# Splitting fp32 weights by whole units: 1024 columns per instruction instead of 512, with the last round and the first stage reordered

## The reference

```python
h = rms_norm(x, norm_w[l])
proj = h @ w_in[l]                                   # 512x2048 @ 2048x6144
q, k, v, g_a, u_p, g_p = jnp.split(proj, [A, 2 * A, 3 * A, 4 * A, 4 * A + P], axis=-1)
attn = diff_attention(q, k, v, ...)                  # two softmaxes per head, p0 - lam * p1
pool = multiscale_pool(u_p, w_pool[l], pool_scale[l])
mixed = jnp.concatenate([attn * jax.nn.silu(g_a), pool * jax.nn.silu(g_p)], axis=-1)
x = x + mixed @ w_out[l]                             # 512x2048 @ 2048x2048
```

## Time and profile before

| what | value |
|---|---|
| median of 3 runs | 789.1 us (788.91 to 791.22) |
| the profiled execution | 789.31 us, span 787.5 us |
| TensorE busy | 775.0 us (98%) |
| VectorE busy | 551.9 us (70%) |
| ScalarE busy | 381.7 us (48%) |
| GpSimd busy | 31.6 us (4%) |
| DMA | 106.22 MB, mean 135 GB/s |

### The profile page before, as it was taken

How to read it: one execution, slowest core, us unless ns; L and a number is a source line. 1 busy time by engine, 2 the same in 40 slices (tenths; PEclk the granted TensorE clock), 3 DMA queues, 4 the chain that set the end, 5 groups by cost and what they waited for, 6 DMA issues and landing times.

```text
span 787.5 us, 9660 instructions
## 1 busy us (share of the span) xinstructions
PE 775.0 (98%) x3470; PEld 638.1 (81%) x3470; DVE 551.9 (70%) x861; ACT 381.7 (48%) x649; POOL 31.6 (4%) x42
## 2 busy tenths in 40 slices
PE   9999999999999999999999999999999889999997
PEld 8878888888888888888888888888788678888886
DVE  5443235887874787785488789458877869887796
ACT  5373234444373444445444437444444756655552
POOL 0010000000000000000000000000000003222200
PEclk9999999999999999999999999999999999999999
DMA  9844323282121336212146322222722169999972
GB/s 333 331 129 132 104 88 101 80 215 77 58 80 54 120 108 173 81 53 81 54 134 154 113 63 71 71 91 80 214 69 66 54 196 266 275 277 264 210 169 107
DMA packets 67079, 106.22 MB, mean 135 GB/s; under 512 B 5344, under 2 KB 46560, under 8 KB 66528
## 3 DMA queue, kind: packets, MB, share of 16 engines
q1 hardware_dynamic: 60288, 86.72, 34.6%
q0 software_dynamic: 4736, 16.78, 10.9%
q10 hardware_dynamic: 2016, 2.18, 0.9%
HBM read 95.17 MB, written 4.19 MB: 126 GB/s over the span
## 4 chain that ended last, share of the span: by engine, by line
PE 85%; DVE 5%; ACT 4%; DMA 3%; SPq 2%; issue 1%; POOL 0%; DVEq 0%; ACTq 0%; POOLq 0%
PE ps L460 83%; DMA raw<-in_w_in 2%; PE ps L587 2%; PE ps L455 1%; ACT probs L807 1%; DMA q_stack<-q_low 1%; SPq L291 1%; DVE probs L1049 1%; ACT at_hi L662 1%; DVE w_lo L907 1%; ACT diff L815 0%; DVE diff L1097 0%; DVE probs L1047 0%; DVE wp_lo L1100 0%; DVE h_lo L934 0%
## 5 line engine op out<-in xcount | busy, mean ns | idle before, releaser
L907 DVE TENSOR_TENSOR w_lo<-raw,w_hi 128x512 fp32r<-128x512 f32 x240 | 163.1, 688 | 167.0 <-ACT w_hi L688 91.3
L460 PE MATMUL ps<-h_hi,w_hi 128*128 128x512 f32 x640 | 251.0, 392 | 0.0
L460 PE MATMUL ps<-h_lo,w_hi 128*128 128x512 f32 x640 | 249.4, 390 | 0.0
L460 PE MATMUL ps<-h_hi,w_lo 128*128 128x512 f32 x640 | 171.2, 389 | 0.0
L688 ACT CAST w_hi<-raw 128x512 fp32r<-128x512 f32 x149 | 90.4, 620 | 161.5 <-PE ps L460 160.7
L460 PEld LDWEIGHTS ps<-h_hi,w_lo 128*128 128x128 f32 x640 | 120.1, 188 | 25.1
L460 PEld LDWEIGHTS ps<-h_hi,w_hi 128*128 128x128 f32 x640 | 120.1, 188 | 24.7
L460 PEld LDWEIGHTS ps<-h_lo,w_hi 128*128 128x128 f32 x640 | 120.2, 188 | 24.6
L460 PE MATMUL ps<-w_hi,h_hi 128*128 128x512 f32 x352 | 122.4, 392 | 2.4 <-DVE h_lo L934 1.3
L460 PE MATMUL ps<-w_hi,h_lo 128*128 128x512 f32 x352 | 121.4, 389 | 0.0
L460 PE MATMUL ps<-w_lo,h_hi 128*128 128x512 f32 x352 | 121.4, 389 | 0.0
(11 more groups left out here) (143 smaller groups left out, 790.0 us busy)
## 6 DMA issues: line engine op xcount, KB each, us to landing
raw<-in_w_in SPq DMA_DIRECT2D x96, 512.0 KB, 3.6
raw<-in_w_out SPq DMA_DIRECT2D x12, 512.0 KB, 3.7
raw<-in_w_out POOLq DMA_DIRECT2D x12, 512.0 KB, 17.2
wide_b<-in_w_out POOLq DMA_DIRECT2D x12, 512.0 KB, 19.1
x_rows<-in_x SPq DMA_DIRECT2D x4, 1024.0 KB, 13.8
tall<-in_w_out SPq DMA_DIRECT2D x8, 512.0 KB, 13.0
tall<-in_w_out POOLq DMA_DIRECT2D x8, 512.0 KB, 23.1
mixed<-in_x_cols SPq DMA_DIRECT2D x3, 1024.0 KB, 13.3
```

What stands on the lines that cost most here:

```text
L460: last = nc.tensor.matmul(dst, lhs, rhs, start=first and i == 0, stop=final and i == len(pairs) - 1, skip_group_check=True)
L907: nc.vector.tensor_tensor(w_lo[:, slot, :], src, w_hi[:, slot, :].bitcast(F32), ALU.subtract).then_inc(w_lo_ready, 1)
```

## The change

ACT and DVE split a whole unit in one instruction each, 1024 columns wide, into two adjacent slots. In the first stage and the rounds this is done at even steps, for halves m+2 and m+3 (before: at each step for half m+3); ACT waits until all halves before m are used. Both semaphores rise by 2 at once. In the projection it is done at even halves.

Other edits: `WARM` from 22 to 16. SP loads one tile of x rows after each of the units 1 to 4, instead of two after each of the units 0 and 1; `x_stats` in steps 11 to 14 instead of 9 to 12, and DVE's factors at step 15 instead of 14. SP moves k before its wait for unit 6 instead of after it. In the last round the forms of pass 0 come a step earlier on ACT (34 to 36), those of pass 1 at 43 to 45 on ACT and 44 to 46 on DVE (before: 38 to 40 on both), the pool is mixed and its form made in step 41 before the weights' split (before: step 42); the two Silus swap places.

```diff
         def form_count(p, pair):
-            if p < 2:
-                return (7 + p) if pair == KP // 2 - 1 else 3 * p + pair + 1
             return (KP // 2) * p + pair + 1
...
                     load_in(Q, nxt - UNITS, 0)
-                if u < 2:
-                    load_x_row(2 * u)
-                    load_x_row(2 * u + 1)
+                if 1 <= u <= ST:
+                    load_x_row(u - 1)
...
                 for unit in range(UNITS - G_UNITS if last_round else UNITS):
+                    if unit == 6:
+                        move_k(r)
                     if unit in (7, 8):
...
                         load_in(Q, j, r + 1)
-                    if unit == 6:
-                        move_k(r)
...
-            def split_first(n):
-                unit, part = divmod(n, 2)
-                if part == 0:
-                    act.wait_ge(raw_in[unit % RAW_SLOTS], (unit // RAW_SLOTS + 1) * 16)
-                if n >= W_SLOTS:
-                    act.wait_ge(w_used, n - W_SLOTS + 1)
-                nc.scalar.copy(w_hi[:, n % W_SLOTS, :], raw[:, unit % RAW_SLOTS, part * 512:part * 512 + 512]
-                               ).then_inc(w_hi_ready, 1)
+            def split_pair(slot, src):
+                nc.scalar.copy(w_hi[:, slot:slot + 2, :].rearrange("p s n -> p (s n)"), src).then_inc(w_hi_ready, 2)
+            def split_first(unit):
+                act.wait_ge(raw_in[unit % RAW_SLOTS], (unit // RAW_SLOTS + 1) * 16)
+                if unit >= 2:
+                    act.wait_ge(w_used, 2 * unit - 2)
+                split_pair(2 * unit % W_SLOTS, raw[:, unit % RAW_SLOTS, :])
...
-                unit, part = divmod(m, 2)
-                if part == 0:
-                    act.wait_ge(raw_in[unit % RAW_SLOTS],
-                                r * (UNITS // RAW_SLOTS * 16) + (V_UNITS + unit) // RAW_SLOTS * 16 + 16)
-                act.wait_ge(w_used, r * HALVES + before(m) - W_SLOTS + 1)
-                nc.scalar.copy(w_hi[:, m % W_SLOTS, :], raw[:, unit % RAW_SLOTS, part * 512:part * 512 + 512]
-                               ).then_inc(w_hi_ready, 1)
+                unit = m // 2
+                act.wait_ge(raw_in[unit % RAW_SLOTS],
+                            r * (UNITS // RAW_SLOTS * 16) + (V_UNITS + unit) // RAW_SLOTS * 16 + 16)
+                act.wait_ge(w_used, r * HALVES + before(m) - 2)
+                split_pair(m % W_SLOTS, raw[:, unit % RAW_SLOTS, :])
...
                 if p == 0:
-                    u, part = divmod(h, 2)
-                    if part == 0:
-                        act.wait_ge(raw_in[u % RAW_SLOTS], ((IN_HALVES // 2 + u) // RAW_SLOTS + 1) * 16)
-                    src = raw[:, u % RAW_SLOTS, part * 512:part * 512 + 512]
+                    u = h // 2
+                    act.wait_ge(raw_in[u % RAW_SLOTS], ((IN_HALVES // 2 + u) // RAW_SLOTS + 1) * 16)
+                    src = raw[:, u % RAW_SLOTS, :]
                 else:
-                    j, part = divmod(hj, 2)
-                    if part == 0:
-                        act.wait_ge((None, wide_in, wide_added, tall_in, wide_added, tall_added, wide_added)[p][j],
-                                    PASS_LANDED[p])
-                    src = w_tile(p, j)[:, part * 512:part * 512 + 512]
-                act.wait_ge(w_used, IN_HALVES + h - W_SLOTS + 1)
-                nc.scalar.copy(w_hi[:, h % W_SLOTS, :], src).then_inc(w_hi_ready, 1)
+                    j = hj // 2
+                    act.wait_ge((None, wide_in, wide_added, tall_in, wide_added, tall_added, wide_added)[p][j],
+                                PASS_LANDED[p])
+                    src = w_tile(p, j)
+                act.wait_ge(w_used, IN_HALVES + h - 2)
+                split_pair(h % W_SLOTS, src)
...
                             nc.scalar.copy(q_stack[rows, c, h], wk(0)[rows, h]).then_inc(qk_hi_ready, 1)
-                    if not last_round or m + 3 < 8 + HALVES - G_HALVES:
-                        split_high(m + 3, r)
-                    else:
-                        split_form_w(m - 37 if m < 41 else 2 * m - 78)
+                    if last_round and m == 41:
+                        form_high(0, KP // 2 - 1)
+                    if m % 2 == 0 and (not last_round or m < 38):
+                        split_high(m + 2, r)
+                    elif last_round and m in (38, 40):
+                        split_form_w(m - 38)
+                    elif last_round and m >= 41:
+                        split_form_w(2 * m - 78)
                     if m == 10:
...
                         nc.scalar.copy(wp_hi, wp_raw[:, :]).then_inc(wp_hi_ready, 1)
-                    if last_round and 35 <= m < 38:
-                        form_high(0, m - 35)
+                    if last_round and 34 <= m < 37:
+                        form_high(0, m - 34)
                     if m == 40:
...
                         nc.scalar.preload_act_table(ACT.Silu)
-                        act.wait_ge(evacuated, r * 3 + 1 + START)
-                        nc.scalar.activation(gate[:, :, :], gate[:, :, :], ACT.Silu).then_inc(gate_ready, 1)
                         act.wait_ge(evacuated, r * 3 + 3 + START)
                         nc.scalar.activation(wk(0), wk(0), ACT.Silu).then_inc(pool_gate_ready, 1)
+                        nc.scalar.activation(gate[:, :, :], gate[:, :, :], ACT.Silu).then_inc(gate_ready, 1)
                         nc.scalar.preload_act_table_set(LN_EXP)
...
                         squares(head_out[:, :], hsq_hi, ps[:, OB, :])
-                    if last_round and 38 <= m < 41:
-                        form_high(1, m - 38)
+                    if last_round and 43 <= m < 46:
+                        form_high(1, m - 43)
                     if m == 42:
                         rstd(head_out[:, :], ps[:, S0, :], 2 * HEAD_DIM, r * 4 + 3)
-                    if last_round and m == 42:
-                        form_high(0, KP // 2 - 1)
                     if m == 46:
...
                                        ).then_inc(pool_placed, 1)
-                    if last_round and m >= 41:
-                        split_form_w(2 * m - 77)
...
                 x_high(q)
-                split_first(2 * q)
-                split_first(2 * q + 1)
+                split_first(q)
             for n in range(1, HALVES):
...
                     nc.scalar.activation(lam_exp[:, :], lam_sum[:, :], ACT.Exp).then_inc(lam_exped, 1)
-                split_first(n + 3)
-                if 9 <= n <= 12:
-                    x_stats(n - 9)
+                if n % 2 == 0:
+                    split_first(n // 2 + 1)
+                if 11 <= n <= 14:
+                    x_stats(n - 11)
                 if KT < n <= KT + ST:
...
                         nc.scalar.copy(corner_part(b), ps[:, OUT_BANKS[1][b], :]).then_inc(first_copied, 1)
-                split_form_w(h)
+                if h % 2 == 0:
+                    split_form_w(h)
                 if hj in (4, 7, 10, 13) and p + 1 < PASSES:
...
                 dve.wait_ge(w_hi_ready, count)
-                nc.vector.tensor_tensor(w_lo[:, slot, :], src, w_hi[:, slot, :].bitcast(F32), ALU.subtract
-                                        ).then_inc(w_lo_ready, 1)
-            def raw_half(n):
-                return raw[:, (n // 2) % RAW_SLOTS, (n % 2) * 512:(n % 2) * 512 + 512]
+                nc.vector.tensor_tensor(w_lo[:, slot:slot + 2, :].rearrange("p s n -> p (s n)"), src,
+                                        w_hi[:, slot:slot + 2, :].rearrange("p s n -> p (s n)").bitcast(F32),
+                                        ALU.subtract).then_inc(w_lo_ready, 2)
+            def raw_pair(n):
+                return raw[:, (n // 2) % RAW_SLOTS, :]
             def split_low(m, r):
-                split_rest(m % W_SLOTS, raw_half(m), r * HALVES + before(m) + 1)
+                split_rest(m % W_SLOTS, raw_pair(m), r * HALVES + before(m) + 2)
...
                 p, hj = divmod(h, P_HALVES)
-                src = raw_half(h) if p == 0 else w_tile(p, hj // 2)[:, (hj % 2) * 512:(hj % 2) * 512 + 512]
-                split_rest(h % W_SLOTS, src, IN_HALVES + h + 1)
+                src = raw_pair(h) if p == 0 else w_tile(p, hj // 2)
+                split_rest(h % W_SLOTS, src, IN_HALVES + h + 2)
...
                                                        op0=ALU.mult, op1=ALU.add).then_inc(attn_ready, 1)
-                    if not last_round or m + 3 < 8 + HALVES - G_HALVES:
-                        split_low(m + 3, r)
-                    else:
-                        split_form_low(m - 37 if m < 41 else 2 * m - 78)
-                    if last_round and 35 <= m < 38:
-                        form_low(0, m - 35)
+                    if last_round and m == 41:
+                        mix_pool(lambda c: wk(2)[:, c, :])
+                    if m % 2 == 0 and (not last_round or m < 38):
+                        split_low(m + 2, r)
+                    elif last_round and m in (38, 40):
```

(27 more changed lines are left out.)

## The result

The changed kernel takes 809.19 us (median of 4 runs, 808.16 to 810.07) beside 789.0 for the kernel before on the same chip: ratio 1.0253, 95% interval 1.0231 to 1.0275. It is 20.2 us slower. The forecast of 800.5 had the direction right and the size too small (11.35 us were forecast); the time lies 1.7 us above its range. The profiled execution has a span of 806.9 us, 19.4 more than before, at a granted clock of 1.00.

What follows compares the result with a forecast made beforehand. TensorE, busy 98% of the span, was taken as the bound, so lost lead counts. Lost 10.6 + 1.3 + 5.2, gained 1.9 + 0.75 + 3.1: net +11.35 us on a 787.5 span gave 800.5 us, range 793.5 to 807.5.

Steps and rivals of the forecast that it cites:

- steps 8 to 22: Rounds: late pairs and work behind them stall TensorE in five steps, 2.66 us a round, 10.6 in four.
- step 20: Rounds: pair (20, 21), subtracted behind the rotation of q head 0, comes late; 1.2 us a round with restart.
- step 22: Rounds: pair (22, 23), subtracted behind q_low and the rotation of head 1, comes late; 0.6 us a round.
- first stage: Start of the kernel: shorter warm-up and x rows no longer ahead of weight units gain 1.9 us.
- q move: Round 3: `move_k` before unit 6's wait lets the late q move come earlier, gaining 0.75 us with restart.
- In steps 24 to 37 ... the pair is never last: nothing.: Rounds: VectorE has under 5 us of work per 6.8 us, so pairs there cost nothing.
- step 38: Rounds 0 to 2: a pair cast heads the chain to the probabilities and delays it 0.43 us, 1.3 in all.
- 2.55 of the 2.72 us there are. With nothing else in the way it just holds.: Output passes: a pair with no other work in its way is split within the time available, so no stall.
- The late pairs: Passes 2 to 6: pairs behind three or four other VectorE operations stall TensorE 0.32 to 0.93 us each, 5.2 in all.
- the passes stall at every pair: Rival, output passes: a pair instruction or handoff 0.3 us longer makes 48 pairs late; near 808 us, chance 0.15.
- the last round: Final round: the new order cuts its stalls from 7.5 to 4.4 us, with six late places left; gain 3.1 us.
- The test that was named: Whole kernel: prediction wrong if TensorE's idle time does not rise by about 9 us or more.

Runs made afterwards that it cites:

- halves in place of pairs: Changed kernel, but each engine uses two 512-wide instructions with a semaphore step each at each pair's place: 793.87 us, ratio 1.0064.
- order only: Changed kernel with all its moves, but weights still split by halves with three halves of lead: 780.74 us, ratio 0.9896.
- pairs only: Changed kernel with the edits of the first stage, of `move_k` and of steps 34 to 47 undone: 815.05 us, ratio 1.0324.
- the kernel with all three edits: Changed kernel with pairs before rotations (steps 18 to 22), pairs behind exponentials (26 to 36), low-part wait at the passes' third product: 795.58 us.
- pairs in the passes alone: Reordered kernel with halves, but pairs in output passes 1 to 6: 790.52 us, ratio 1.0023.

## Why the prediction was right or wrong

**Right: the lead, not the work, decides.** The prediction read from the earlier trace rows that cheaper instructions win nothing and that a pair loses one half of lead. The halves in place of pairs show it, with 15 us for the first half alone, and order only shows that nothing was to be won from VectorE's time.

**Right: steps 8 to 22.** 2.66 us a round forecast, 2.85 measured; step 20 1.2 and 1.28, step 22 0.6 and 0.6. The chain behind the earlier trace rows was walked through correctly, and moving the pairs ahead of the rotations took the stalls of steps 20 and 22 away.

**Right in number: first stage and q move.** -1.9 and -1.83; -0.75 and -0.75. Both are in part luck. In the six other kernels with the same first stage, that stage gave between -1.0 and -2.3 us. And the q move is in time with pairs alone as well, where `move_k` stands as before; so in the changed kernel the gain can't be put down to the earlier `move_k`. With halves (order only) the gain is there too; `move_k` was not tried by itself.

**Wrong: "In steps 24 to 37 ... the pair is never last: nothing."** The pair is not last, but on ScalarE it stands in front of the exponentials and makes them 0.43 us later, so that they end just when the scores want them: 0.06 us before the score is due, where it was 0.52 before (181.17 for 181.69). About 1.0 us a round, 3.9 in all, half of the miss. The step asked only whether the split itself is late, not what stands behind it; step 38 was asked that question and answered with 0.43, where 0.22 was measured.

**Wrong: "2.55 of the 2.72 us there are. With nothing else in the way it just holds."** Two terms of that chain were too small: 0.28 us instead of 0.20 from TensorE's start to the cast, and 0.10 instead of 0.03 from the cast to the subtraction. Both had been read at instructions of 512 columns. The signal came when the matmul was due, not 0.17 us before. And the load of the weights, which wants 0.12 us ahead, was put at nothing. By the rows above, the 0.17 us of the forecast would have been enough for it. The late pairs lost what was forecast (5.1 and 5.2), the plain pairs 2.7 instead of nothing: 7.9 us in the passes instead of 5.2. The rival "the passes stall at every pair", near 808 with a chance of 0.15, had the place right. It asked for a handoff 0.3 us longer; the two handoffs were 0.15 us longer, and that this was already enough is due to the load.

**Too large: the last round,** -3.1 forecast and -1.9 measured. All six late places are those that were listed. TensorE was late there by 0.86, 0.99, 0.75, 0.60, 0.81 and 0.74 us, where 0.7, 1.0, 0.45, 0.4, 0.4 and 0.8 were forecast: the two pairs were sized rightly, and the waits for the probabilities and the heads were 1.0 us too small together. Why was not tried. Waiting later for the low part gave back 1.0 us, at the pairs (4, 5) and (18, 19).

Sum of the misses: 3.9 + 0.8 (steps 8 to 22) - 0.6 (step 39) + 2.65 + 1.2 = 8, of the 8.1 between 11.35 and 19.5. The test that was named, TensorE idle for 9 us or more longer, failed at 7.2 although the loss was larger: the signals that were just too late count as busy, and so do the restarts.

## What to carry to other kernels

In a ring of buffers, a larger instruction pays with lead: its first part is ready with its last and it needs all its slots free. Where the engine that it relieves is not the bound, that is only cost; take the new order and keep the small instructions (780.7 us here, 1.0% faster than before, where both together were 2.5% slower).

Give each wait ahead of a matmul the room of one weight load (0.12 us here), and put it ahead of the first matmul that reads the data, not of the group. Read handoffs at instructions of the size that the new kernel will have. To find waits without that room, look at distances between starts and at PEld, not at idle time. And whatever is moved behind one deadline must be checked against the next: of 3.5 us won at the scores 2.8 were lost at the transposes.

## What the hardware showed beyond that

A late signal costs TensorE 0.11 us beyond the wait, and up to that with no wait at all, where the weight load starts less than 0.12 us before its matmul is due. VectorE started 0.10 us behind a cast of 1024 columns and 0.03 us behind one of 512.

Three waits in the last round were each followed by over 3 us at a granted clock of 0.50, about 1.5 us lost each time: 2.47 and 1.89 us in pairs only, 1.85 us in the kernel with all three edits. Waits of 1.83, 1.97 and 2.42 us in three other kernels were not. No length of the wait before it tells the two apart.

The last unit of w_out that SP loads took 6.4 us from issue to landing in the kernel before, 8.3 in the changed kernel, 8.9 in order only and 10.7 with pairs in the passes alone. ScalarE waited 3.1 and 4.5 us for it in the last two; in the changed kernel it shows no such wait.
